# Block two's gates: eight block-diagonal products on 128 rows against pairs of products on 64 rows

## The reference, cut to what matters

```python
def rg_lru(x, w_a, b_a, w_x, b_x, lam):
    xb = x.reshape(B, S, RNN_BLOCKS, RNN_BW)          # 16 blocks of 64 channels
    r = sigmoid(einsum('bsnc,ncd->bsnd', xb, w_a).reshape(B, S, C) + b_a)
    i = sigmoid(einsum('bsnc,ncd->bsnd', xb, w_x).reshape(B, S, C) + b_x)
    log_a = -RG_C * r * softplus(-lam)
    a = exp(log_a)
    mult = sqrt(-expm1(2.0 * log_a))
    u = mult * (i * x)
    ...                                               # h_t = a_t h_{t-1} + u_t
```

## Time and profile before

| | |
|---|---|
| median of 3 runs | 2306.16 us (2306.08 to 2306.39) |
| the profiled execution | 2306.12 us |
| its span, first to last instruction | 2304.3 us |
| TensorE busy | 2272.0 us, 99% |
| VectorE busy | 1570.7 us, 68% |
| ScalarE busy | 1322.7 us, 57% |
| records of the gate products | 64, from 1219.6 and from 1883.0 us |

### The profile page before, as it was taken

One profiled execution on the slowest core, in us unless ns is written; L12 is line 12 of the kernel. 1 busy time (PEld: TensorE's weight loads), 2 busy tenths in 40 slices (PEclk: granted clock), 3 DMA queues, 4 the chain that ended last, 5 costly groups with the idle time before them and its releaser, 6 DMA issues.

```text
span 2304.3 us, 31105 instructions
## 1 busy us (share of the span) xinstructions
PE 2272.0 (99%) x13028; PEld 1995.5 (87%) x13028; DVE 1570.7 (68%) x1797; ACT 1322.7 (57%) x1801; POOL 42.7 (2%) x76
## 2 busy tenths in 40 slices
PE   8999999999999999999999999999999999999998
PEld 8888888888998988888898888888888898988886
DVE  6866776479766775667577766664776578666755
ACT  6675655476755654655458645554554458555544
POOL 1000000010000000010000000000100000000000
PEclk9999999999999999999999999999999999999999
DMA  7715555556245655465555455555655645455553
GB/s 224 230 61 183 188 190 195 185 181 224 92 149 181 212 191 192 165 216 188 186 184 165 128 183 190 185 191 193 195 195 182 204 153 165 147 183 181 184 192 119
DMA packets 323515, 411.92 MB, mean 179 GB/s; under 512 B 11600, under 2 KB 245456, under 8 KB 323376
## 3 DMA queue, kind: packets, MB, share of 16 engines
q1 hardware_dynamic: 318160, 394.68, 52.6%
q0 software_dynamic: 4928, 14.26, 2.0%
q10 hardware_dynamic: 288, 0.99, 0.1%
HBM read 408.85 MB, written 1.05 MB: 178 GB/s over the span
## 4 chain that ended last, share of the span: by engine, by line
PE 75%; DVE 14%; ACT 9%; issue 1%; DMA 0%; SPq 0%; DVEq 0%; ACTq 0%
PE banks L602 19%; PE banks L610 10%; PE banks L679 9%; PE banks L681 9%; PE banks L680 9%; DVE lo L1743 7%; ACT hi L1168 5%; PE banks L586 3%; PE banks L587 3%; PE banks L588 3%; DVE mg L1889 1%; PE banks L730 1%; DVE mg L1793 1%; PE banks L863 0%; PE banks L667 0%
## 5 line engine op out<-in xcount | busy, mean ns | idle before, releaser
L1743 DVE TENSOR_TENSOR lo<-raw,hi 128x2048 fp32r<-128x2048 f32 (+1 forms) x382 | 858.6, 2251 | 566.1 <-ACT hi L1168 565.7
L1168 ACT ACTIVATE hi<-raw 128x2048 fp32r<-128x2048 f32 (+1 forms) x382 | 715.3, 1876 | 221.5 <-DMA raw<-in_ffn_w_out 85.4
L602 PE MATMUL banks<-x_in,hi 128*128 128x512 f32 x2304 | 538.0, 390 | 0.7 <-issue 0.6
L602 PEld LDWEIGHTS banks<-x_in,hi 128*128 128x128 f32 x2304 | 427.5, 188 | 87.5 <-issue 1.2
L610 PEld LDWEIGHTS banks<-x_in,lo 128*128 128x128 f32 x2304 | 286.6, 192 | 6.9 <-issue 0.9
L610 PE MATMUL banks<-x_in,lo 128*128 128x256 f32 x2304 | 289.6, 283 | 0.8 <-issue 0.6
L586 PE MATMUL banks<-x_in,hi 128*128 128x256 f32 x736 | 210.5, 286 | 0.0
L588 PE MATMUL banks<-x_in,lo 128*128 128x256 f32 x736 | 208.2, 283 | 0.0
L587 PE MATMUL banks<-x_in,hi 128*128 128x256 f32 x736 | 208.2, 283 | 0.0
L679 PE MATMUL banks<-hi,x_hid 128*128 128x512 f32 x528 | 206.0, 390 | 0.0
L681 PE MATMUL banks<-hi,x_hid 128*128 128x512 f32 x528 | 205.5, 389 | 0.0
(11 more groups left out here) (338 smaller groups left out, 3102.2 us busy)
## 6 DMA issues: line engine op xcount, KB each, us to landing
raw<-in_w_in SPq DMA_DIRECT2D x108, 1024.0 KB, 5.2
raw<-in_ffn_w_in SPq DMA_DIRECT2D x88, 1024.0 KB, 5.1
raw<-in_w_ffn_in SPq DMA_DIRECT2D x44, 1024.0 KB, 5.1
raw<-in_ffn_w_out SPq DMA_DIRECT2D x40, 1024.0 KB, 5.1
raw<-in_w_ffn_out SPq DMA_DIRECT2D x20, 1024.0 KB, 5.1
raw<-in_w_o_gla SPq DMA_DIRECT2D x8, 1024.0 KB, 5.1
raw<-in_w_o_attn SPq DMA_DIRECT2D x8, 1024.0 KB, 5.2
raw<-in_w_out SPq DMA_DIRECT2D x8, 1024.0 KB, 5.1
```

The source lines that it names most:

```text
L602: mm = pe.matmul(bank[b + f], wh[:, k, f * P:(f + 1) * P], x[:, k, :, :].rearrange("p n s -> p (n s)"), start=(start and k == 0), stop=(k ...
L1168: act_fn(high, of, ACT.Copy).then_inc(hi_done.up(), 1)
L1743: tt(rest, of, parts(tile, hi)[0].bitcast(F32), ALU.subtract).then_inc(lo_done.up(), 1)
```

## The change

The weights are laid side by side in place of block-diagonal. For each group f, `bd[0:64, f, :]` holds `w_a` of the lower block in columns 0 to 63 and `w_x` in columns 64 to 127. On partitions 64 to 127 the two are swapped. No zeros are needed. One product now has 64 rows and gives both gates of one 64-channel block. So there are again 16 products of 128 columns of weights in a layer, on 64 rows each, in four groups of two f; the lower blocks (a = 0) go to one bank of a pair and the upper ones (a = 1) to the other. The signal to ScalarE comes once for two f.

After the sigmoids `rr` has gate r of the lower block on partitions 0 to 63 and gate i of the lower block on partitions 64 to 127; `ii` has gate i of the upper block on partitions 0 to 63 and gate r of the upper block on 64 to 127. The r gates are where they belong. The i gates are on the wrong half, and four DMAs in each layer from SBUF to SBUF, issued by ScalarE, move them into a new tile `xi`. Biases are loaded in the same layout (`gate_bias`, four more DMAs by GpSimd).

```diff
-                nc.gpsimd.memset(bd[:], 0.0).then_inc(zeroed.up(), 1)
-                pool.wait_ge(*zeroed.now())
-                pool.sem_inc(pool_go.sem, 1)
                 for i, name in enumerate(("rg_wa_2", "rg_wx_2")):
                     w = dram[name][layer].rearrange("(f a) c d -> a c f d", a=2)
                     for a in range(2):
-                        pool.dma_start(bd[64 * a:64 * a + 64, i, :, 64 * a:64 * a + 64], w[a]).then_inc(par_in.up(), 16)
+                        at_col = 64 * (i ^ a)
+                        pool.dma_start(bd[64 * a:64 * a + 64, :, at_col:at_col + 64], w[a]).then_inc(par_in.up(), 16)
                 pool.dma_start(pk2[:], dram["pack2"][layer]).then_inc(par_in.up(), 16)
+                for i in range(2):
+                    for a, c in enumerate((P2_BA, P2_BX) if i == 0 else (P2_BX, P2_BA)):
+                        pool.dma_start(gate_bias[64 * a:64 * a + 64, i, :],
+                                       dram["pack2"][layer, 64 * i:64 * i + 64, c:c + KD]).then_inc(par_in.up(), 16)
...
+        rg_banks = ((2, 3), (4, 5), (6, 7), (1, 0))
...
-                pe.wait_ge(*par_in.at(8))
-                for f in range(KD):
-                    b = 4 + f % 4
-                    pe.wait_ge(*conv_ready.next())
-                    take(b)
-                    for i in range(2):
-                        mm = pe.matmul(bank[b][:, i * S:(i + 1) * S], bd[:, i, f, :], y[:, f, :],
-                                       start=True, stop=True)
+                pe.wait_ge(*par_in.at(12))
+                for m in range(KD // 2):
+                    pe.wait_ge(*conv_ready.next(2))
+                    take(*rg_banks[m])
+                    for f in (2 * m, 2 * m + 1):
+                        for a in range(2):
+                            lanes = slice(64 * a, 64 * a + 64)
+                            mm = pe.matmul(bank[rg_banks[m][a]][:, f % 2 * S:(f % 2 + 1) * S], bd[lanes, f, :],
+                                           y[lanes, f, :], start=True, stop=True)
                     mm.then_inc(rg_full.up(), 1)
-                    freed[b] = rg_ev.next()
+                    freed[rg_banks[m][0]] = freed[rg_banks[m][1]] = rg_ev.next(2)
...
                 for f in range(KD):
-                    act.wait_ge(*rg_full.next())
-                    for i, (to, c) in enumerate(((rr, P2_BA), (ii, P2_BX))):
+                    if f % 2 == 0:
+                        act.wait_ge(*rg_full.next())
+                    for i, to in enumerate((rr, ii)):
                         done = rg_ev if i else act_step
-                        act_fn(to[:, f, :], bank[4 + f % 4][:, i * S:(i + 1) * S], ACT.Sigmoid,
-                               bias=pk2[:, c + f:c + f + 1]).then_inc(done.up(), 1)
+                        act_fn(to[:, f, :], bank[rg_banks[f // 2][i]][:, f % 2 * S:(f % 2 + 1) * S], ACT.Sigmoid,
+                               bias=gate_bias[:, i, f:f + 1]).then_inc(done.up(), 1)
+                    if f % 4 == 3:
+                        act.wait_ge(*act_step.now())
+                        act.wait_ge(*rg_ev.now())
+                        act.dma_start(xi[0:64, f - 3:f + 1, :], rr[64:128, f - 3:f + 1, :]).then_inc(shift_in.up(), 16)
+                        act.dma_start(xi[64:128, f - 3:f + 1, :], ii[0:64, f - 3:f + 1, :]).then_inc(shift_in.up(), 16)
...
+                act.wait_ge(*shift_in.at(4))
                 act_fn(rr[:], la[:], ACT.Exp, scale=-1.0).then_inc(act_step.up(), 1)
...
-                dve.wait_ge(*rg_ev.at(KD))
-                tt(la[:], rr[:], sp[:, 4, :].unsqueeze(2).broadcast_to([P, KD, S]), ALU.mult).then_inc(lru_v.up(), 1)
-                step(tt(ii[:], ii[:], y[:], ALU.mult))
+                for f in (0, 4):
+                    dve.wait_ge(*rg_ev.at(f + 4))
+                    for a, of in enumerate((rr, ii)):
+                        lanes, fs = slice(64 * a, 64 * a + 64), slice(f, f + 4)
+                        tt(la[lanes, fs, :], of[lanes, fs, :], sp[lanes, 4, fs].unsqueeze(2).broadcast_to([64, 4, S]),
+                           ALU.mult).then_inc((lru_v if f and a else dve_step).up(), 1)
+                dve.wait_ge(*dve_step.now())
+                dve.wait_ge(*lru_v.now())
+                dve.wait_ge(*shift_in.at(4))
+                step(tt(ii[:], xi[:], y[:], ALU.mult))
                 pump(BY2["q"][0].index + 2)
```

More of the change, by code:

```diff
@@ L41 @@
 TOTALS = {
-    "const_in": (0, 0), "first_row": (0, 0), "ident_in": (0, 0), "up_in": (9, 0), "rope_in": (6, 0), "par_in": (0, 8), "pt_in": (1, 1), "row_in0": (1, 1), "row_in1": (2, 2),
-    "row_in2": (1, 1), "row_in3": (1, 1), "row_used": (5, 5), "layer_done": (1, 1), "zeroed": (0, 1),
+    "const_in": (0, 0), "first_row": (0, 0), "ident_in": (0, 0), "up_in": (9, 0), "rope_in": (6, 0), "par_in": (0, 12), "pt_in": (1, 1), "row_in0": (1, 1), "row_in1": (2, 2),
+    "row_in2": (1, 1), "row_in3": (1, 1), "row_used": (5, 5), "layer_done": (1, 1), "zeroed": (0, 0),
     "hi_done": (78, 114), "lo_done": (78, 114),
-    "tile_used": (78, 114), "act_step": (81, 81), "dve_step": (145, 101), "alpha_abs": (4, 0), "x_loaded0": (0, 0),
+    "tile_used": (78, 114), "act_step": (81, 81), "dve_step": (145, 104), "alpha_abs": (4, 0), "x_loaded0": (0, 0),
     "x_loaded1": (0, 0), "h_ready": (12, 16), "first_rows": (3, 4), "squared": (8, 0), "rt_ready": (10, 8),
@@ L57 @@
     "mg_act": (8, 16), "mg_f": (4, 4), "mg_hi": (4, 4), "mg_lo": (4, 4), "conv_ready": (0, 8),
-    "rg_full": (0, 8), "rg_ev": (0, 8), "lru_v": (0, 4), "lru_a": (0, 3), "f_v": (0, 1), "f_a": (0, 1),
+    "shift_in": (0, 4), "rg_full": (0, 4), "rg_ev": (0, 8), "lru_v": (0, 4), "lru_a": (0, 3), "f_v": (0, 1), "f_a": (0, 1),
     "fbh_ready": (0, 1), "y_hi": (0, 1), "y_lo": (0, 1), "out_done": (0, 0), "pool_go": (0, 0),
@@ L305, in build_program @@
         pt = at("pt", [P, 2, S], o_pt)
-        bd = at("bd", [P, 2, KD, P], o_par)
+        bd = at("bd", [P, KD, P], o_par)
+        gate_bias = at("gate_bias", [P, 2, KD], o_par + 4 * KB)
         pk2 = at("pk2", [P, P2_END], o_pk + 64)
@@ L317, in build_program @@
         rxp = at("rxp", [P, KD, S + 3], o_s1)
+        xi = at("xi", [P, KD, S], o_s1)
         fz = at("fz", [P, S], o_s1 + 9 * KB)
@@ L381, in build_program @@
         sum_in, half_ev = signal("sum_in"), signal("half_ev")
+        shift_in = signal("shift_in", 16)
         out_done = signal("out_done", 16)
@@ L1613, in _ @@
                 pump(BY2["rx"][2].index + 2)
-                act.wait_ge(*par_in.at(8))
+                act.wait_ge(*par_in.at(12))
                 act.wait_ge(*lru_v.at(1))
@@ L2269, in _ @@
                 residual(BY2["ffn1_out"], [(2, 3), (0, 1)], half_root, 1, by_features, x_in)
-                dve.wait_ge(*par_in.at(8))
+                dve.wait_ge(*par_in.at(12))
                 step(nc.vector.memset(rxp[:, :, 0:3], 0.0))
```

## The result

| | before | after |
|---|---|---|
| median of 4 runs each, us | 2306.12 (2306.07 to 2306.39) | 2320.57 (2320.50 to 2321.25) |
| ratio to before, 95% interval | | 1.0063 (1.0046 to 1.0081) |
| span of the profiled execution, us | 2304.3 | 2318.7 |
| stall of TensorE at q[2], layers one and two, us | 0.32, 0.31 | 8.05, 7.70 |
| first gate record to q[2], us | 18.31, 18.31 | 23.51, 23.19 |

The account below looks back on a forecast made before the run. ScalarE's and VectorE's chain to `lo` of q[2], not TensorE, was taken to bound the kernel. Terms of 0.1 + 0.9 + 0.1 + 0 = +1.1 us a layer, +2.2 us for two, gave 2308.3 us, range 2305.0 to 2312.7.

Parts of the forecast that it names:

- What bounds q[2]: At q[2], ScalarE and VectorE set the start through `lo`; TensorE's earlier work, gates included, has 0.32 us to spare.
- The gates: TensorE's 64-row gate products overlap at 0.105 to 0.134 us each, saving 2.4 to 3.4 us a layer.
- Rival 3: At the gates, 64-row products don't overlap and stay at 6.72 us: 1.84 us a layer, 2309.8 us; chance 0.08.
- First signal and `la`: Ahead of q[2], ScalarE's signal after eight records and VectorE's `la` cut into four operations: +0.1 us each per layer.
- ScalarE's stop: Mid-sigmoids, ScalarE waits for its own last sigmoid and issues two DMAs: +0.9 us a layer, bounds +0.18 to +1.5.
- The transfers: The product ahead of q[2]'s `lo` waits for the four copies, landing in time: 0 us, far end +3.8.
- rival 2: Beside k[0]'s load the transfers land late, `lo` of q[2] 1.9 us later a layer: 2312.1 us; chance 0.08.
- Rival 1: TensorE's clock falls in q[2]'s 4.0 us stall, losing 1.7 to 2.6 us each; chance 0.30, both layers 0.13.
- The three small terms: Ahead of q[2], first signal, ScalarE's stop and `la`: 0.1, 0.9 and 0.1 us a layer.
- Rival 4: At q[2] the saving is kept, needing a shorter first signal or sigmoid run: 2.6 us a layer, 2300.9; chance 0.04.

Follow-up runs that it names:

- e2: Changed kernel without the four transfers, ScalarE's stop and the waits; the product reads `ii`, so i gates stay unmoved: 2309.82 us, ratio 1.0015.
- e4: Changed kernel with 56 transposes of a constant keeping TensorE busy ahead of q[2]: 2316.72 us, ratio 1.0047.
- e11: Changed kernel with the four transfers issued by SyncE ahead of k[0]'s load, instead of by ScalarE: 2309.75 us, ratio 1.0014.
- e5: Changed kernel with SyncE's load of k[0] held back until the four transfers have landed: 2315.11 us, ratio 1.0038.
- e12: e9 with VectorE's `lo` for the first tile of the values moved ahead of the second half of the scans: 2300.33 us, ratio 0.9974.
- e9: e7 with `lo` of k[1] to k[3] ahead of other VectorE work and ScalarE's `hi` of k[2] earlier: 2306.12 us, ratio 0.9998.
- e1: Changed kernel with VectorE's wait for the transfers and the `xi` product moved from ahead of `lo` of q[2] to later: 2314.71 us, ratio 1.0039.
- e3: Kernel before plus the same four transfers from ScalarE into an unused tile, and the waits for them: 2310.62 us, ratio 1.0017.
- e7: Changed kernel with transfers on SyncE ahead of k[0]'s load, q[2] and q[3] prepared early, the product late: 2310.64 us, ratio 1.0020.
- e8: e7 without the transfers, the product reading `ii`, so the i gates stay unmoved: 2311.32 us, ratio 1.0021.

## Why the prediction was wrong, point by point

- **What bounds q[2].** Right. The saving of TensorE became a stall, released by VectorE's `lo`, and e2 shows that it was worth nothing as it stood. One reading on the way was wrong: a sigmoid every 0.36 us is faster than a product every 0.42 (6.72 / 16). ScalarE stays behind the products because of the 1.28 us of table load ahead of its first sigmoid, and nothing in the sum hangs on it.
- **The gates.** Right, at the lower bound: 24 records show as 2.86 us and 8 as 1.14, so (2.86 - 1.14) / 16 = 0.107 each against 0.21, a full overlap of two. The Trainium skill (TensorEngine Tiling (Array Packing), Theoretical Speedup) gives a factor of up to two, and the trace agrees. The wait for bank 0 was 0.34 us, inside "up to 0.6". Rival 3 fell.
- **First signal and `la`.** 1.22 us from the first gate record to the table load against 1.10: +0.12, and +0.17 for `la` (1232.12 against a last sigmoid that ended at 1229.62, 2.50; 2.33 before). The forecast had 0.1 and 0.1.
- **ScalarE's stop.** Right in kind, too small: the ninth sigmoid came 1.80 us after the eighth, 0.36 before, so +1.44, where the forecast had 0.9 and the bounds ended at 1.5. In layer two it was 2.06, so +1.70, above the bound. The issues of layer one took 0.51 and 0.61 us in place of the 0.34 read from one issue at the program's start.
- **The transfers. This step failed.** "I take 0" rested on a landing of 5.1 us beside k[0]'s load, on the very edge. The last transfer took 8.2 and 7.7 us. At q[2] that is 5.20 - (0.12 + 1.44 + 0.17) = +3.5 us in layer one and 4.88 - (0.12 + 1.70 + 0.17) = +2.9 us in layer two. The mechanism, the moment (1229.5 foreseen, 1229.81 found) and the far end of the bound (+3.8) were all in the text, and rival 2 had a chance of 0.08 and 1.9 us. A median of loads that have the engines to themselves was used as the price of two that share them. By the Trainium skill (DMA: Bandwidth & Descriptors, Issuing engines are not separate DMA queues) they interleave; the trace agrees, with 8.9 us for the load in place of 5.1 and 8.2 for the transfer in place of 3.7.
- **Rival 1, the clock. The forecast had this at nothing too.** It came true in both layers and on top of rival 2; e4 puts it at 3.9 us, and the forecast had 1.7 to 2.6 us a stall. The error was to give "both layers" a chance of 0.13 and to treat the rivals as exclusive. It didn't need the late transfers: the clock fell in both layers of e2, e11 and e5, where none was late, behind stalls of 2.96 to 5.73 us, and the forecast itself foresaw a stall of 4.0. By e5 the change with its transfers in time is 9.0 us slower than before, so the late landing is 5.5 of the 14.4 us, and ScalarE's stop and the clock alone would have broken the range. The landing weighs less in the time (5.5) than at q[2] (3.5 + 2.9) since half pace cost less behind the longer stall (1.6 us in layer two after, 2.6 in e5): in the changed kernel a part of it passed while TensorE stood idle. The three small terms as measured (1.7 and 2.0), both layers' transfers and the clock give 2306.1 + 3.7 + 6.4 + 3.9 = 2320.1 us, 0.5 below the result.
- **Rival 4, the saving kept.** Not in the change as made. But its sentence that the chain of sigmoids would have to be shorter was wrong. e12 keeps that chain as it is, puts `lo` and `hi` of the tiles ahead of other work, and gains 5.9 us. How near the two outcomes lie shows in e9: one stall of 1.8 us in each layer, six tiles behind q[2], and one fall of the clock behind it undid the gain.

Not settled: why an issue on ScalarE's queue twice took 1.8 to 2.0 us (e1 and e5, one of eight in each), why ScalarE's stop is 0.25 us longer in layer two (e3 and e5 have it too), and why stalls of 1.8 to 2.2 us left the clock alone in some layers and not in others.

## What to carry to other kernels

When an engine's work gets shorter and its next wait is already released by another engine, ask what its earlier progress sets off: here it released a buffer sooner, and the load for it landed on the new transfers. Price a transfer on which a chain waits as if the next load ran beside it, and keep it off the queue of an engine in the chain; behind a stall of 3 us add the clock, since such costs come together. A saving on a busy engine is had only when each tile behind it is prepared that much sooner, one stall after the other: here q[2], k[1] and the first tile of the values.

## What the runs showed of the hardware that was not expected

- TensorE's granted clock fell to its lower level at every one of the 14 stalls of 2.96 to 8.05 us behind dense work (after, e1, e2, e5, e7, e8, e11, both layers each). It also fell after 1.96 us in one layer of e3 and 1.84 us in one of e9, 1.2 and 1.4 us after the work had gone on, while 1.71 (e3), 1.80 (e9), 1.61 and 2.20 us (e4) left it alone. Half pace lasted 3.4, 6.8 or 10.2 us by the clock records, the longest behind the 8.05 us stall.
- A copy of 256 KB from SBUF to SBUF landed in 3.0 to 4.4 us where no load of 1 MB was issued ahead of it. With such a load issued between or just ahead of the second pair it took 5.6 to 8.3 us, and the load 6.8 to 8.9 in place of 5.1 (after, e1, e4). With the load issued 1 us behind the copies (e7, e9, e11, e12) they kept 3.1 to 3.9 us, and the load took 6.1 to 6.7.
- An issue of such a copy took 0.46 to 0.64 us of ScalarE's or SyncE's time, but for the two of 1.8 and 2.0 us.
